# Starting addresses of four operand buffers, shifted against each other by 16, 32, 48 and 16 bytes

## What is computed

```
h    = rms_norm(x, attn_norm[l])
proj = h @ w_in[l]                      # 2048 wide in, 3648 out
...                                     # three kinds of attention on proj
x    = x + mixed @ w_o[l]               # 2048 x 2048
h    = rms_norm(x, mlp_norm[l])
x    = x + square(relu(h @ w_up[l])) @ w_down[l]    # 2048 x 8192, 8192 x 2048
```

## Time and profile before

| | |
|---|---|
| median of three runs | 3119.89 us |
| lowest, highest | 3118.1, 3120.46 us |
| span of the profiled execution | 3119.2 us |
| TensorE matmuls busy | 3099.6 us, 99% |
| weight loads busy (beside matmuls) | 2659.7 us, 85% |
| VectorE, ScalarE, GpSimd busy | 59%, 47%, 23% |
| granted TensorE clock | 0.998 of 2.4 GHz |
| DMA | 598 MB, mean 192 GB/s |

### The profile page before, as it was taken

One profiled execution on the slowest core, in us unless ns is written; L12 is line 12 of the kernel. 1 busy time (PEld: TensorE's weight loads), 2 busy tenths in 40 slices (PEclk: granted clock), 3 DMA queues, 4 the chain that ended last, 5 costly groups with the idle time before them and its releaser, 6 DMA issues.

```text
span 3119.2 us, 45296 instructions
## 1 busy us (share of the span) xinstructions
PE 3099.6 (99%) x16368; PEld 2659.7 (85%) x16368; DVE 1839.2 (59%) x2369; ACT 1465.8 (47%) x2274; POOL 719.0 (23%) x746
## 2 busy tenths in 40 slices
PE   8999999999999999999999999999999999999999
PEld 7888888888888888888888888889888888888887
DVE  5676655555555567665555555567686555555554
ACT  5454544444345545454453444552565434444443
POOL 1422241231411143042314150115030101001010
PEclk9999999999999999999999999999999999999999
DMA  6534565655655554455556465657433555555554
GB/s 241 189 142 164 189 219 189 219 189 188 219 189 211 192 187 152 164 182 213 192 188 219 185 219 189 224 213 275 171 120 142 189 199 189 195 192 188 189 188 162
DMA packets 66640, 598.04 MB, mean 192 GB/s; under 512 B 14320, under 2 KB 24816, under 8 KB 31424
## 3 DMA queue, kind: packets, MB, share of 16 engines
q1 hardware_dynamic: 54912, 588.17, 51.7%
q10 hardware_dynamic: 11184, 5.49, 0.7%
q0 software_dynamic: 400, 2.44, 0.2%
HBM read 577.93 MB, written 18.15 MB: 191 GB/s over the span
## 4 chain that ended last, share of the span: by engine, by line
PE 95%; DVE 2%; DMA 1%; ACT 1%; issue 1%; ACTq 0%; DVEq 0%
PE bank L671 93%; DMA urow<-us 1%; PE bank L783 1%; DVE w_lo L1723 1%; PE bank L942 0%; ACT w_hi L1209 0%; PE bank L831 0%; DVE sb L2243 0%; DMA par<-params 0%; DMA u<-urow 0%; DVE w_lo L1717 0%; DVE gbuf L2208 0%; DVE ks L2186 0%; ACT act_hi L1559 0%; DVE act_lo L2216 0%
## 5 line engine op out<-in xcount | busy, mean ns | idle before, releaser
L671 PE MATMUL bank<-xg,w_hi 128*128 128x512 f32 (+1 forms) x4256 | 1434.4, 385 | 1.7 <-issue 1.7
L671 PE MATMUL bank<-xg,w_lo 128*128 128x256 f32 (+1 forms) x4064 | 1142.8, 281 | 0.0
L671 PEld LDWEIGHTS bank<-xg,w_hi 128*128 128x128 f32 x4256 | 789.6, 188 | 168.4 <-issue 2.3
L1717 DVE TENSOR_TENSOR w_lo<-raw,w_hi 128x1024 fp32r<-128x1024 f32 x512 | 668.1, 1341 | 439.4 <-ACT w_hi L1220 439.1
L1220 ACT ACTIVATE w_hi<-raw 128x1024 fp32r<-128x1024 f32 x512 | 514.0, 1052 | 634.4 <-PE bank L671 634.4
L671 PEld LDWEIGHTS bank<-xg,w_lo 128*128 128x128 f32 x4064 | 765.4, 188 | 0.9
L671 PE MATMUL bank<-w_hi,act_hi 128*128 128x512 f32 x1920 | 752.5, 392 | 0.2 <-issue 0.2
L671 PE MATMUL bank<-w_hi,act_lo 128*128 128x512 f32 x1920 | 747.7, 389 | 0.0
L671 PE MATMUL bank<-w_lo,act_hi 128*128 128x512 f32 x1920 | 747.2, 389 | 0.0
L1723 DVE TENSOR_TENSOR w_lo<-raw,w_hi 128x1024 fp32r<-128x1024 f32 x510 | 626.0, 1234 | 170.4 <-ACT w_hi L1209 169.4
L1209 ACT ACTIVATE w_hi<-raw 128x1024 fp32r<-128x1024 f32 x514 | 514.4, 1052 | 174.8 <-PE bank L671 147.6
(11 more groups left out here) (346 smaller groups left out, 2014.9 us busy)
## 6 DMA issues: line engine op xcount, KB each, us to landing
raw<-stream SPq DMA_DIRECT2D x260, 2048.0 KB, 7.7
stabs<-ssm_tabs SPq DMA_DIRECT2D x8, 1176.0 KB, 9.7
rdo<-stabs SPq DMA_DIRECT2D x8, 768.0 KB, 7.3
ssm_bc<-smat SPq DMA_DIRECT2D x8, 640.0 KB, 11.7
raw<-stream SPq DMA_DIRECT2D x4, 1024.0 KB, 8.6
stabs<-ssm_f SPq DMA_DIRECT2D x8, 512.0 KB, 10.8
drv<-stabs SPq DMA_DIRECT2D x8, 512.0 KB, 5.6
trig<-stabs SPq DMA_DIRECT2D x8, 408.0 KB, 5.9
```

The costliest lines, as they stand in the source:

```text
L671: return pe.matmul(o, a, b, start=start, stop=stop, skip_group_check=True)
L1717: dve.tensor_tensor(flat_lo[j][:, 1024 * h:1024 * h + 1024], flat_raw[r][:, 2048 * j + 1024 * h:2048 * j + 1024 * h + 1024], flat_hi[j][:, ...
```

## The change

A helper `skewed` places a tile with a number of spare values ahead of it and returns the view behind them. `w_hi1` and `act_lo` get 4 values (16 bytes) of lead, `w_lo0` none, `w_lo1` 4, and each placement that has a lead pushes what follows by 32 bytes. From the code, against the kernel before:

| tile | moved by, bytes | modulo 64 |
|---|---|---|
| `raw0`, `raw1`, `w_hi0` | 0 | 0 |
| `w_hi1` | 16 | 16 |
| `w_lo0` | 32 | 32 |
| `w_lo1` | 48 | 48 |
| `x`, `xg`, `act_hi` | 64 | 0 |
| `act_lo` | 80 | 16 |
| `par`, `tab`, small tiles, regions from `free_at` on | 96 | 32 |

`ACT_HALF` is written out so that it keeps its value, and `unread`, the target of a 128-byte dummy DMA, moves to another region to make room. No instruction, wait or order changes, only addresses.

```diff
-    hi = [place(f"w_hi{i}", [P, KT, P], F32R) for i in range(2)]
-    lo = [place(f"w_lo{i}", [P, KT, P], F32R) for i in range(2)]
+    def skewed(name, shape, skew):
+
+        n = int(np.prod(shape[1:]))
+        t = place(name, [P, n + skew], F32R)
+        return t[:, skew:skew + n].rearrange("p (k n) -> p k n", k=shape[1])
+
+    hi = [skewed(f"w_hi{i}", [P, KT, P], 4 * i) for i in range(2)]
+    lo = [skewed(f"w_lo{i}", [P, KT, P], 4 * i) for i in range(2)]
...
-    act_hi = place("act_hi", [P, KT, S], F32R)
-    act_lo = place("act_lo", [P, KT, S], F32R)
+    act_hi = skewed("act_hi", [P, KT, S], 0)
+    act_lo = skewed("act_lo", [P, KT, S], 4)
     act_end = at[0]
-    ACT_HALF = (act_end - act_at) // 2
+    ACT_HALF = 4 * KT * S
...
-    unread = place("unread", [P, 32], where=region)
...
     sb0 = place("sb0", [P, 384], where=region)
+    unread = place("unread", [P, 32], where=region)
```

## The result

The changed kernel takes 3148.26 us (median of four runs) against 3118.99 us for the kernel before in four runs beside it.

What follows compares the result with a forecast made beforehand. It took back-to-back TensorE matmuls, busy 99% of the span, as the bound. 15.4 + 3.8 + 0 = 19.2 us on 3119.2 gave 3138.4, with the median 0.7 higher 3139 us; range 3098 to 3163.

Steps and rivals of the forecast that it cites:

- The steps of line 671 are all that can change: TensorE matmuls busy in 99% of the span; addresses act above all in matmul-to-matmul steps, with 191 us of excess at stake.
- Wide, 4.0 ns on 3840 and 2.0 on 1920, 19.2 us: 512-column matmuls: 15.4 us where stream and load now differ modulo 64, 3.8 us elsewhere; at most 23 us slower.
- the half for the 1920: Wide matmuls alike modulo 64 but with act_hi moved 64 bytes: half of 4.0 ns each, 3.8 us.
- The leads are the cause: Leads make 3840 wide matmuls stream from another place modulo 64 than their load: 15.4 of the 19.2 us.
- Paired, 0: 3872 pairs of 512 and 256 columns: no change; bounds 20 us slower to 62 us of gain.
- the mixed price: Pairs already pay for varied places, as xg walks through all eight places modulo 512; hence 0 us.
- The shift by itself costs nothing: Operands begun at 16, 32 or 48 modulo 64: nothing seen at half rate, not shown free at full rate.
- No difference: Rival: 16-byte lines stay whole and streams pass all places of their loads anyway; 3120 us, chance 0.20.
- Faster: Rival: distinct quarters of 64 bytes keep stream and load apart on 9648 matmuls; about 3085 us, chance 0.22.
- Much slower: Rival: a beginning off 64 costs the stream at every matmul, 23 + 20 = 43 us; 3163 us, chance 0.12.
- The last chain longer by 5 us: Final unbroken piece of line 671, 704 us, stays one piece and grows by about 5 us.
- The wide step at 229 to 231 ns, the pair at 349 to 351: Expected profile: 512-column step up from 226.8 ns in most runs, and the time of a 512-and-256-column pair.

Runs made afterwards that it cites:

- The leads alone: Changed kernel with its four leads kept, but x, xg and act_hi 256 bytes further on in place of 64; 3147.37 us, ratio 1.0091 against the kernel before.
- the push of 64 bytes: Kernel before with 64 bytes put ahead of x, moving xg, act_hi and act_lo on, weight buffers unmoved; 3155.04 us, ratio 1.0113.
- the loop: Kernel of only matmul pairs of 512 and 256 columns, moving operand walking with xg's 1088-byte pitch; 349.2 ns a pair begun at 0.
- the loop kernel: Kernel of only back-to-back fast fp32 matmuls, whole computation left out, starts of moving and stationary operand shifted; 226.7 ns best for 512 columns, mostly 228.4 to 235 elsewhere.
- the table: Steps of 512-column matmuls alone, moving or stationary operand shifted 0 to 496 bytes by 16; 226.7 ns at 0, mostly 228.4 to 235 elsewhere.

## Why the prediction was right, point by point

- *The steps of line 671 are all that can change.* Right. Counts of matmuls and loads, clock and the busy time of VectorE and ScalarE stayed, and steps account for 29 of 29.3 us. The cover of VectorE and ScalarE held: ScalarE still waited 655 us for TensorE, where it waited 634.
- *Wide, 4.0 ns on 3840 and 2.0 on 1920, 19.2 us.* The sign was right, and so was the mechanism in its main part, that starting places of stream and load act on each other; the size was too small: 4.4 ns on all 5760, 25 us, above the upper bound of 23. The term that was mis-sized is the half for the 1920 that "stay alike modulo 64" (`w_hi0` streaming): they rose by 5.4 ns in place of 2.0, 10 us for 3.8. The period is 256 bytes, not 64, so they are as far off as the others. That the other 3840 came out at 15 us, as forecast, is luck in part: it is the mean of 5.5 ns with `w_hi1` and 2.4 with `w_lo`, and no row before the change had their distances. Pushed alone, `act_hi` at 64 bytes from every weight buffer costs 6.5 ns, where the earlier trace rows gave 4.0 as a mean over four places modulo 256.
- *The leads are the cause.* Half right. The leads alone cost 28 us; but the push of 64 bytes, which I treated as a remainder, costs 35 alone. The time of the change is not a sum of the two.
- *Paired, 0.* 1.1 ns a pair, 4 us, inside the bounds. In the kernel with the leads alone it was 1.9. To take it as nothing because all pairs pay the mixed price already was nearly right, but not exact: in the loop the walk begun at 32 bytes took 351.7 ns for 349.2.
- *The shift by itself costs nothing.* Right as far as tried: everything 32 bytes on made no difference. Both operands 16 or 48 bytes on in the loop kernel took 230.1 against 227.4 at 32, so a start at an odd multiple of 16 isn't free; why stays open.
- *No difference* fell: with lines of 16 bytes, as in the Trainium skill's "SBUF — State Buffer", section "Specifications (TRN2)", the leads of whole lines should leave the time alone, and they cost 28 us. Its argument that a stream passes all places of its load anyway is refuted by the table, in which the places count though every stream of 2048 bytes is eight times longer than the period.
- *Faster* fell: nothing fast was measured under 226.7 ns for 512 columns, so the 10.6 ns between half and full rate are not there to be won by places. *Much slower* fell as to its cause, a start off 64 that costs the stream at every matmul: everything 32 bytes on cost nothing, and the push of 64 bytes, which leaves no start off 64, cost 35 us. Its terms came out at 25 and 4 us for 23 and 20.
- The two independent read ports of the Trainium skill's "TensorE: Matmul & The Clock Gate", section "Step-by-step: what each phase is for", don't agree with these runs: a stream's step depends on where the operand being loaded beside it begins, 226.8 ns or 233.3 with the stationary operand 64 bytes on.
- *The last chain longer by 5 us.* It went from 704.12 to 712.02 us, 8; four wide runs of 384 at 4.4 ns are 7 of them.
- *The wide step at 229 to 231 ns, the pair at 349 to 351.* 231.2, just above, and 350.4.

## What to carry to other kernels

Where fast fp32 matmuls stand back to back, the addresses of the streamed and the loaded operand are a tuning knob of up to 3.5% of the step. For matmuls of 512 columns, keep both at multiples of 32 bytes and at the same place modulo 256, or measure, and look at every tile that a new lead or pad pushes along behind it. For pairs of 512 and 256 columns the same place was not reliably the best (346.7 or 353.5 ns), and 16 bytes on with a pitch of 1024 was, in four kernels. Two runs of the same instruction with different operands, already in the profile, show whether the knob exists and roughly what it is worth (4.0 ns there, 4.4 to 6.5 in the end). Compare long unbroken runs of starts, not spans, when a DMA wait elsewhere comes and goes.

## What the runs showed of the hardware that was not expected

- The step of a 512-column fp32r matmul has a period of 256 bytes in the starting place of either operand, 226.7 ns at the same place, up to 234.7 elsewhere and 235.8 at 4 bytes. At multiples of 32 the distance decides, at odd multiples of 16 the place itself too. Plain fp32 shows nothing of it (215.8 ns a record of 256 columns at three distances).
- Even at the best places a fast matmul costs 13 ns over its columns, at 256 as at 512 columns.
- The same places modulo 256 can give two steps, 346.7 or 353.3 ns a pair and 226.7 or 233.3 ns for 512 columns, each held through a whole stretch. What decides between them, and what lies behind 256 bytes, wasn't settled: the runs show the period, not its cause.
- A DMA that took 14.3 us or more, against 13.3 or less in the other profiles, left TensorE idle for 2.5 us; its granted clock then stood at half for 10.2 us, though matmuls followed without a gap. It is the estimated 7.6 us between the two groups of times that most versions of the kernel have.
